# GpSimd's key selection cut into pieces, with the low half of an early expert tile between two pieces

## The reference, cut to what matters

```python
sc = jnp.einsum("thpk,hpnk->thpn", q, sub_keys)        # (512, 8, 2, 128)
s_top, i_top = lax.top_k(sc, 16)
cand = s_top[:, :, 0, :, None] + s_top[:, :, 1, None, :]
best, pos = lax.top_k(cand.reshape(n_tok, 8, 256), 16)
idx = jnp.take_along_axis(cand_idx.reshape(n_tok, 8, 256), pos, axis=-1)
g = jax.nn.softmax(best, axis=-1)
...
act = jax.nn.gelu(jnp.einsum("phkd,pd->phk", u_tab[ib], tb))
```

## Time and profile before

| | us |
|---|---|
| median of 3 runs | 2267.18 |
| the runs | 2265.44 to 2270.49 |
| the profiled execution, its own time | 2266.39 |
| its span in the profile | 2264.6 |
| mean granted TensorE clock, share of full speed | 0.971 |
| PE busy | 2114.8 (93%) |
| DVE busy | 1695.0 (75%) |
| ACT busy | 813.8 (36%) |
| POOL busy | 778.4 (34%) |

### The profile page before, as it was taken

One profiled execution on the slowest core, in us unless ns is written; L12 is line 12 of the kernel. 1 busy time (PEld: TensorE's weight loads), 2 busy tenths in 40 slices (PEclk: granted clock), 3 DMA queues, 4 the chain that ended last, 5 costly groups with the idle time before them and its releaser, 6 DMA issues.

```text
span 2264.6 us, 35855 instructions
## 1 busy us (share of the span) xinstructions
PE 2114.8 (93%) x11175; PEld 1864.5 (82%) x11175; DVE 1695.0 (75%) x3348; ACT 813.8 (36%) x1408; POOL 778.4 (34%) x677
## 2 busy tenths in 40 slices
PE   7998888569999998988999999999999999999997
PEld 5876677557888877878999999999998888888886
DVE  3776554648777765699788888888846888888887
ACT  4454322322322232324444444444433333333333
POOL 2000044000000000278588898898812222222221
PEclk9998999789999999999999999999999999999999
DMA  6744000133252404303478898998768999999995
GB/s 132 93 56 45 13 1 0 48 104 77 72 130 67 127 35 157 113 20 116 168 247 278 295 313 278 310 303 270 256 234 301 349 338 336 340 336 336 339 336 200
DMA packets 229809, 428.42 MB, mean 189 GB/s; under 512 B 18500, under 2 KB 155876, under 8 KB 229476
## 3 DMA queue, kind: packets, MB, share of 16 engines
q1 hardware_dynamic: 171956, 254.38, 37.4%
q0 software_dynamic: 41472, 151.01, 19.5%
q10 hardware_dynamic: 16304, 22.08, 2.7%
HBM read 381.28 MB, written 46.14 MB: 189 GB/s over the span
## 4 chain that ended last, share of the span: by engine, by line
PE 49%; DVE 1%; POOL 0%; issue 0%; ACT 0%; POOLq 0%; ACTq 0%; DVEq 0%
PE bank L2072 23%; PE bank L2055 20%; PE bank L2036 4%; PE bank L2044 2%; DVE u_spread L2232 0%; POOL row_slot L1816 0%; DVE v_residual L2220 0%; POOL u_two L1982 0%; DVE u_lo L2189 0%; DVE v_stat L126 0%; DVE v_stat L128 0%; DVE v_stat L130 0%; DVE v_stat L127 0%; DVE v_stat L129 0%; ACT u_weight_lo L2276 0%
## 5 line engine op out<-in xcount | busy, mean ns | idle before, releaser
L2055 PE MATMUL bank<-xt_hi,u_hi 128*128 128x384 f32 x896 | 309.5, 345 | 0.0
L2055 PE MATMUL bank<-xt_hi,u_lo 128*128 128x384 f32 x896 | 300.7, 336 | 0.0
L2055 PE MATMUL bank<-xt_lo,u_hi 128*128 128x384 f32 x896 | 300.3, 335 | 0.0
L2072 PE MATMUL bank<-u_hi,u_one 128*128 128x512 f32 x768 | 299.0, 389 | 1.1 <-DVE u_two L2192 1.1
L2072 PE MATMUL bank<-u_lo,u_one 128*128 128x512 f32 x768 | 298.8, 389 | 0.0
L2072 PE MATMUL bank<-u_hi,u_two 128*128 128x512 f32 x768 | 298.8, 389 | 0.0
L1816 POOL DMA_INDIRECT row_slot<-in_peer_v_dram,row_index x128 | 137.9, 1077 | 420.9 <-DVE row_x L2200 368.7
L2257 ACT ACTIVATE u_hi<-xh 128x1024 fp32r<-128x1024 f32 x128 | 135.9, 1061 | 329.4 <-PE bank L2072 328.9
L2189 DVE TENSOR_TENSOR u_lo<-xh,u_hi 128x1024 fp32r<-128x1024 f32 x128 | 156.8, 1225 | 80.9 <-ACT u_hi L2257 80.9
L1470 POOL TENSOR_TENSOR k_wlo<-q_raw,k_whi 128x2048 fp32r<-128x2048 f32 x4 | 18.7, 4672 | 562.0 <-ACT k_whi L1600 562.0
L1816 POOL DMA_INDIRECT row_slot<-in_peer_u_dram,row_index x128 | 157.5, 1230 | 65.7 <-issue 37.1
(11 more groups left out here) (432 smaller groups left out, 4887.3 us busy)
## 6 DMA issues: line engine op xcount, KB each, us to landing
xh<-in_peer_v_dram SPq DMA_DIRECT2D x128, 512.0 KB, 5.4
xh<-in_peer_u_dram SPq DMA_DIRECT2D x112, 512.0 KB, 4.9
x_raw<-in_w_in_dram SPq DMA_DIRECT2D x56, 512.0 KB, 7.0
v_ga<-acts SPq DMA_DIRECT2D x128, 192.0 KB, 5.4
acts<-xh ACTq DMA_DIRECT2D x110, 192.0 KB
weights<-u_spread POOLq DMA_DIRECT2D x32, 512.0 KB, 6.9
v_gg<-weights SPq DMA_DIRECT2D x128, 128.0 KB, 5.2
p_raw<-in_w_in_dram SPq DMA_DIRECT2D x12, 1024.0 KB, 9.6
```

The lines of the kernel that those rows point to most:

```text
L2055: mm = pe.matmul(k.ps[4 + b][:, 0:DENSE], w[b][:, c, :], x[:, c, 0:DENSE], start=(c == 0 and w is uhi and x is hi), stop=(c == DC - 1 and ...
L2072: mm = pe.matmul(k.ps[q][:, :], h[b][:, t * P:(t + 1) * P], w[b][:, f], start=start and h is hhi and w is vhi, stop=stop and h is hlo, ski ...
```

## The change

GpSimd's order from step 1 on is rewritten. The multiply of a selection is made in two halves of 128 x 1024, and one `low_early` stands behind the first half, one behind the second, and one behind the first fold. Nothing is computed otherwise than before, and no other engine's program changes.

```diff
--- before.py
+++ after.py
@@ -1677,17 +1677,39 @@
                 def low_early(e):
                     pool.wait_ge(u_copied, after(4 * (e + 1)))
                     pool.tensor_tensor(u_lo[e % 4], u_turn[e % 2], u_hi[e % 4].bitcast(F32), ALU.subtract).then_inc(u_low, 1)
-                select(1, 0)
-                for e in range(2):
+                def pick_pairs(i, n, at):
+                    pool.wait_ge(s["matched"], after(2 * i + n + 1))
+                    m = slice(at * pairs // 2, (at + 1) * pairs // 2)
+                    order.add(pool.tensor_tensor(eq[n][:, m, :, :], eq[n][:, m, :, :],
+                                                 keys_of(i)[:, n, m, :].unsqueeze(2).to_broadcast([P, pairs // 2, K, K]), ALU.mult))
+
+                def fold(n, w):
+                    order.wait()
+                    order.add(pool.tensor_tensor(eq[n][:, :, :, 0:w], eq[n][:, :, :, 0:w], eq[n][:, :, :, w:2 * w], ALU.add))
+
+                def close(i, n):
+                    fold(n, 2)
+                    order.wait()
+                    pool.tensor_tensor(sel[:, n, i, :, :], eq[n][:, :, :, 0], eq[n][:, :, :, 1], ALU.add
+                                       ).then_inc(s["reduced"], 1)
+
+                def between(i, n, e):
+                    pick_pairs(i, n, 0)
                     low_early(e)
-                select(1, 1)
-                for e in range(2, 7):
-                    low_early(e)
-                select(2, 0)
-                for e in range(7, 9):
-                    low_early(e)
-                select(2, 1)
-                for e in range(9, EARLY):
+                    pick_pairs(i, n, 1)
+                    low_early(e + 1)
+                    fold(n, 8)
+                    low_early(e + 2)
+                    fold(n, 4)
+                    close(i, n)
+
+                low_early(0)
+                between(1, 0, 1)
+                between(1, 1, 4)
+                low_early(7)
+                between(2, 0, 8)
+                between(2, 1, 11)
+                for e in range(14, EARLY):
                     low_early(e)
 
             @block.vector
```

## The result

| | before | changed |
|---|---|---|
| median, us | 2267.48 (5 runs, 2265.44 to 2273.1) | 2278.41 (5 runs, 2276.07 to 2278.6) |
| the profiled execution, us | 2266.39 | 2278.41 |
| its span, us | 2264.6 | 2276.6 |

The changed kernel takes 1.004 of the time before, 95% interval 1.0025 to 1.0055: 9 us by that ratio. The medians differ by 10.9 us, the two spans by 12.0. The forecast was 2278.

What follows compares the result with a forecast made beforehand. PE and DVE were taken as level at the stage's end, the later one deciding. Step 3's late start 7.7, collisions 0.3, product 15 2.7, transposes 0.6, less 0.25, gave +11 us: 2278, range 2269 to 2285.

Steps and rivals of the forecast that it cites:

- Step 3 starts +7.7 late: DVE's step 3 starts at 1053.3 instead of 1045.59 us, held by POOL's late second selection of step 1; bounds +3.6 to +8.6.
- the semaphore of the close: DVE's wait, ahead of step 2's comparisons, for POOL to finish step 1's second selection, due at 1046.4 us instead of 1029.0.
- The gap of 7 us ahead of the comparisons: Expected sign in the changed profile: DVE idle about 7 us ahead of L1772 of step 2, released by POOL.
- the wait at low 3: POOL waits 1.7 us for tile 3, copied only behind the gelu of product 0; bounds 0 and 2.4.
- low 7: Low half right behind step 1's close on POOL, probably taking the port before DVE's comparisons of step 2: +2.4 us.
- The short instructions are blocked too: DVE's eleven short instructions, L1751 to L1765, also block on the port; priced in step 3 at +2.5 us, bounds 0 and 6.
- Port collisions in step 3, +0.3 in all: Net change from DVE and POOL sharing the port in step 3: +0.3 us, range used -4 to +6.
- Cast and sums: DVE's cast and three sums in step 3 take 7.1 us against 6.1 before, +1.0; bounds 4 and 8.5.
- comparisons: DVE's comparisons of step 3, 6.71 us before and 4.5 when POOL is through: -1.0 us, bounds -2.2 and 0.
- first multiply: DVE's first multiply behind the comparisons of step 3, 4.50 us before against 2.28 for the second: -2.2 us.
- Product 15 and its transposes, +3.3: PE's last work of the stage, slowed by a lower clock after idling: +2.7 us for product 15, +0.6 for the transposes.
- shorter pieces pay: Rival: POOL holds the port 2.4 us at a time instead of 4.6 and PE's gaps go; 2260 us, chance 0.08.

Runs made afterwards that it cites:

- e4_own_masks: Changed kernel with the masks of step 2 in memory of their own, so DVE's comparisons there no longer wait for step 1's close; 1.0031 of the kernel before.
- e7_busy_pe: Changed kernel with 90 more matmuls of unused output on PE, between product 14 and its wait for the chosen indices; 1.0026 of the kernel before.
- e1_halves_only: Selections of steps 1 and 2 cut into pieces as in the changed kernel, but no low half between the pieces; 0.9996 of the kernel before.
- e2: Changed kernel's low halves inside the selections of step 1 only, with whole selections in step 2 as before; 1.0001 of the kernel before.
- e3: Changed kernel's low halves inside the selections of step 2 only, with step 1 as in the kernel before; 1.002 of the kernel before.
- e6: Changed kernel with own masks for step 2, and POOL pausing in selection (1,1) until both comparisons of step 2 are done; 1.004 of the kernel before.

## Why the prediction was right, and where it was not

- **What bounds the stage** (PE and DVE level, the later of them releases product 15): right. PE's waits for low halves fell by 7.0 us and nothing came of it.
- **Step 3 starts +7.7 late:** measured +6.9 (1055.16 less 2.67, against 1045.59). The size held, the step behind it failed. The prediction put the wait on the semaphore of the close ("DVE stands ready at about 1039"). DVE was not ready then: it was inside its short instructions until 1048.1, on the port, and e4_own_masks shows that taking the semaphore away changes nothing. The gap of 7 us ahead of the comparisons, which the prediction named as its sign, is not in the trace. The two gave nearly the same number because both end with POOL's chain. The reckoning of that chain was good, but not within its bounds: the close was due at 1046.4, at the earliest 1044.7, and came at 1044.5 (1047.21 less 2.67), mostly since the wait at low 3, put at 1.7, was not seen. That low 7 would take the port ahead of DVE was right. Behind it four short instructions, 1.2 us, still had to run, which gave back part of the early close; that part is luck.
- **The short instructions are blocked too:** right, and larger than thought; the prediction priced it in step 3 alone, and step 2 is where it cost 7 us and more. It also held that no row of before could show it. One does: in step 3 the first of them took 0.25 us, and not 0.17, and ended with the low half that POOL had begun at 1072.12:

```profile
1078.99 0.25 DVE L1751 COPY k_largest<-k_best 128x8 f32<-128x8 f32 x1
```

```profile
1072.12 7.10 POOL L1679 TENSOR_TENSOR k_wlo<-q_raw,k_whi 128x1024 fp32r<-128x1024 f32 x3
```

The Trainium skill ("SBUF — State Buffer", Terms, the shared port pair) has it that the pair is held for a full instruction and the loser fully blocks. By that rule, the trace agrees where the copy took 1.47 us in e7_busy_pe and ended with POOL's instruction. Where it took 7.41 us across several POOL instructions, the trace shows more than that.
- **Port collisions in step 3, +0.3 in all:** measured +0.3, by terms that missed and cancelled. Cast and sums +3.4 (9.53 us against 6.14; forecast +1.0), short instructions +1.35 (3.89 against 2.54; forecast +2.5), comparisons -2.2 (forecast -1.0), first multiply -2.2 (as forecast).
- **Product 15 and its transposes, +3.3:** measured +2.2, and e7_busy_pe shows that the clock is the whole of it. Product 0's 6.92 us was too high a guide; the lower bounds, 1.6 from product 7 and 0.5 for the transposes, were nearer.
- **The sum:** the stage lost 9.3 us where +11 was forecast. That the time met 2278 to 0.4 us is in part luck: the median of the five is the profiled execution, which had another 2.7 us of scatter ahead of the stage, and the first median of before was 2 to 3 us below its later ones. A forecast of +9 would have been the better one of this stage.
- **The rivals:** "shorter pieces pay" is out. Pieces alone are worth nothing (e1_halves_only), and low halves between them lengthen the chains that shut DVE out.

What stays open: whether the two parts (e2, e3) cost less alone than together, and why, is argued from their timelines and lies at the edge of the intervals. What decides whether DVE gets the port between two POOL instructions was not settled either. It is not how far POOL's instruction had come: the copy began 0.96 to 0.98 us into a low half in four kernels, and took 7.4 us in two (changed, e4_own_masks) and 1.5 in two (e2_step1_only, e7_busy_pe).

## What to carry to other kernels

Before filling GpSimd's pauses, ask who uses them: here they were VectorE's way to the port, and GpSimd work without a pause turned a copy of 0.17 us into one of 7.4. Where two engines are level at the end of a stage, freeing one gives nothing; look first at what the engine that serves it (here GpSimd) then does to the other. Put independent work between dependent pieces only if no engine needs the gap that the dependence leaves.

## What the runs showed that was not expected

- An instruction that waits for the shared port counts as busy: DVE showed 49.3 of 50 us busy before and after, with up to 7 us of it in a copy of 8 columns. The group's own duration against its nearest twin is the view that shows it, not the waits.
- Several POOL instructions in a row can pass over one waiting DVE instruction (7.41, 7.40 and 8.22 us, over POOL instructions of 2.4). In all three it was served where a POOL instruction needed the result of the one just ahead of it.
- Not every DVE instruction is caught: the sixteen MAX8 (128x128 each) that began at 1066.98 under POOL's unbroken work took 3.19 us, and 3.18 or 3.19 before. Copies, casts, TENSOR_SCALAR and TENSOR_TENSOR were the ones that grew.
- Removing the semaphore (e4), or the semaphore and the port conflict of one phase (e6), moved 0 and 9.9 us locally and nothing clear of noise in total. GpSimd had 38 to 41 us of work in each 50, and every place to which it was moved here met VectorE again or held up PE.
